# q/k/v and 48-column projections in three rounded passes, with norm sums taken token by token

## The reference

```python
m = silu(c) @ w_mod + b_mod                      # six rows of 1024: shift, scale, gate, twice
h = rms_norm(x, norm1) * (1 + scale) + shift     # latent rows by c, context rows by c_ctx
p = h @ w_in                                     # q k v z | a b | gq gk gv gg | lr
# head group A, gated DeltaNet, 4 heads of 128
q, k, v = split(silu(conv1d_centred(p[qkv], w[3])))
q = q * rsqrt(sum(q*q) + 1e-6) * 128 ** -0.5     # sums over the 128 channels of a head
k = k * rsqrt(sum(k*k) + 1e-6)
# ... chunked scans forward and backward, context first; GLA is head group B ...
x = x + gate1 * (concat(y_a, y_b) @ w_out)
x = x + gate2 * conv_ffn(modulate(rms_norm(x, norm2)))
out = rms_norm(x, final_norm)
```

## Time and profile before

| | |
|---|---|
| median of 3 runs | 1615.28 us (1615.0 to 1617.74) |
| the profiled execution, its own time | 1616.57 us |
| its span, first to last instruction | 1614.8 us |
| mean granted TensorE clock | 0.988 of full speed |
| TensorE, VectorE, ScalarE, GpSimd busy | 97%, 79%, 37%, 31% of the span |
| DMA | 215 MB, mean 133 GB/s |

### The profile page before, as it was taken

The page is one execution under the profiler, slowest core; times in us unless marked ns, Lnnn a source line. Parts: engine busy times, 40 slices in busy tenths (PEclk is TensorE's granted clock), DMA queues, the critical chain, the costliest instruction groups (busy, mean ns, idle before and its releaser), DMA issues.

```text
span 1614.8 us, 20799 instructions
## 1 busy us (share of the span) xinstructions
PE 1572.9 (97%) x8010; PEld 1171.0 (73%) x8010; DVE 1273.6 (79%) x1861; ACT 589.8 (37%) x984; POOL 495.5 (31%) x483
## 2 busy tenths in 40 slices
PE   7999999999999989999999999999999999999997
PEld 2455554987489966565578888888888888788886
DVE  5488878499866678888787389889889888967658
ACT  2544333553243312323464432222222222344455
POOL 5001101121143345656313633433434433600001
PEclk9999999999999989999999999999999999999999
DMA  9276553865398740100433246444352511233365
GB/s 348 74 254 215 179 188 127 255 174 128 93 271 252 210 170 14 27 14 26 148 128 108 88 124 124 124 95 139 75 141 78 119 53 29 88 133 97 101 147 169
DMA packets 216031, 214.99 MB, mean 133 GB/s; under 512 B 41221, under 2 KB 156239, under 8 KB 215708
## 3 DMA queue, kind: packets, MB, share of 16 engines
q1 hardware_dynamic: 200144, 183.97, 36.7%
q0 software_dynamic: 9392, 26.48, 7.5%
q10 hardware_dynamic: 6396, 3.20, 0.7%
HBM read 171.50 MB, written 65.19 MB: 147 GB/s over the span
## 4 chain that ended last, share of the span: by engine, by line
PE 55%; DVE 6%; issue 1%; ACT 1%; POOL 1%; DMA 0%; ACTq 0%; DVEq 0%; POOLq 0%
PE PS L2257 10%; PE PS L2255 10%; PE PS L2259 10%; PE PS L2113 4%; PE PS L2292 4%; PE PS L2294 4%; PE PS L2293 4%; PE PS L2128 3%; DVE Qbd L2587 2%; PE PS L2215 1%; PE PS L2217 1%; PE PS L2216 1%; PE PS L2150 1%; DVE AT L2603 1%; DVE Ex L2568 0%
## 5 line engine op out<-in xcount | busy, mean ns | idle before, releaser
L2758 DVE SCALAR_TENSOR_TENSOR acc<-PS,fcol,acc 128x945 f32<-128x945 f32 (+2 forms) x176 | 215.1, 1222 | 29.2 <-ACT acc L2380 23.7
L2758 DVE SCALAR_TENSOR_TENSOR act<-PS,fcol,act 128x945 f32<-128x945 f32 (+2 forms) x176 | 215.1, 1222 | 21.6 <-ACT act L2380 16.2
L2255 PE MATMUL PS<-h2hi,whi 128*128 128x512 f32 x704 | 219.5, 389 | 0.0
L2259 PE MATMUL PS<-h2hi,wlo 128*128 128x512 f32 x704 | 219.4, 389 | 0.0
L2257 PE MATMUL PS<-h2lo,whi 128*128 128x512 f32 x704 | 219.3, 389 | 0.0
L2024 POOL TENSOR_TENSOR wlo<-wu,whi 128x1024 fp32r<-128x1024 f32 x44 | 106.4, 2423 | 214.1 <-ACT whi L2373 214.0
L425 PE MATMUL PS<-hT,wq 128*128 128x512 f32 (+1 forms) x432 | 163.1, 537 | 0.0
L2259 PEld LDWEIGHTS PS<-h2hi,wlo 128*128 128x128 f32 x704 | 132.1, 188 | 27.5
L2257 PEld LDWEIGHTS PS<-h2lo,whi 128*128 128x128 f32 x704 | 132.1, 188 | 27.4
L2255 PEld LDWEIGHTS PS<-h2hi,whi 128*128 128x128 f32 x704 | 132.1, 188 | 27.4
L425 PEld LDWEIGHTS PS<-hT,wq 128*128 128x128 f32 x432 | 81.6, 190 | 78.4 <-issue 75.6
(11 more groups left out here) (336 smaller groups left out, 2981.0 us busy)
## 6 DMA issues: line engine op xcount, KB each, us to landing
wm<-in_w_mod_dram SPq DMA_DIRECT2D x24, 1024.0 KB, 7.6
wu<-in_w_up_dram SPq DMA_DIRECT2D x44, 512.0 KB, 3.9
t_sums<-in_w_down_dram POOLq DMA_DIRECT2D x12, 1024.0 KB, 9.9
raw<-t_sums SPq DMA_DIRECT2D x44, 256.0 KB, 2.6
raw<-in_w_down_dram SPq DMA_DIRECT2D x33, 256.0 KB, 2.7
wq<-in_w_in_dram SPq DMA_DIRECT2D x12, 512.0 KB, 8.9
gdn_x_image<-ztile SPq DMA_DIRECT2D x10, 516.0 KB, 9.9
gdn_xt_image<-ztile SPq DMA_DIRECT2D x10, 516.0 KB, 8.0
```

The source lines that it names most:

```text
L2255: pe.matmul(PS[:, b + half, :], whi[k][u][:, kk, :], h2hi[:, 4 * half:4 * half + 4, kk, :], start=(kk == 0), stop=False)
L2259: mm = pe.matmul(PS[:, b + half, :], wlo[k][u][:, kk, :], h2hi[:, 4 * half:4 * half + 4, kk, :], start=False, stop=(kk == KT - 1))
L2758: tp = v.scalar_tensor_tensor(out=t_[:, r0:r1, c0:c1], in0=up[:, r0 + dr:r1 + dr, c0 + dc:c1 + dc], scalar=tap_col(j, k, f), in1=t_[:, r0: ...
```

## The change

1. `hT` is no longer built in place. Each tile of h is staged in one of three buffers `hs`, stored to DRAM by SP (`h_out`), rounded by ScalarE into `hhi`, and the rest is subtracted into `hlo`, by VectorE for tiles 0 to 3 and by GpSimd for 4 to 9. A tile reuses the buffer of the tile three before it and waits for its store.
2. The weights of q, k, v and of lrab are split in the same way, `w_high` on ScalarE and `w_low` on GpSimd. Each fp32 matmul becomes three in fp32r (`three`).
3. The product stays in PSUM. ScalarE writes the centre tap from there (`centre`), VectorE adds the two other taps straight from PSUM. The large `raw` buffers go.
4. The squares are summed by using them as weights against one column of ones, in fp32: token sums as a [128, 8] or [128, 10] table (`sums`). Root, reciprocal and turn work on that table; the turned row is stored to DRAM and read back to all partitions (`spread`, on SP). The turn of q's table sits in the v product, that of k's in the next head's q product, after the first 512 columns.
5. v is copied per head into `vst` and stored by ScalarE's queue.
6. The rest of the modulation goes in 32 parts of two steps (0.5 MB each), with two small accumulators that are spilled one by one.
7. At the start of the second stage SP loads ten tiles of `hT` back (5.2 MB) ahead of its other transfers, and the first value weights have their own buffer `wgA`. The third stage loads `hL` in twelve transfers instead of three.

```diff
+                def h_out(t):
+                    sp.wait_ge(s_hta, 2 + t + 1)
+                    sp.wait_ge(s_htv, 2 + t + 1)
+                    sp.dma_start(hT_dram[t], hs[t % 3][:, :, :]).then_inc(s_hst[t % 3], 16)
...
+                def spread(kind, h):
+                    n = NT if kind else NL
+                    sp.wait_ge(s_bank[kind], h + 2)
+                    sp.dma_start(r_dram[kind, h, 0:n, :], nrow[kind][0:n, :]).then_inc(s_nrs[kind], 16)
+                    sp.wait_ge(s_nrs[kind], 16 * (h + 1))
+                    if kind:
+                        sp.wait_ge(s_un[0], h + 1)
+                    elif h:
+                        sp.wait_ge(s_un[1], h)
+                    sp.dma_start(crn[:, 0:n * P], r_dram[kind, h, 0:n, :].rearrange("t p -> (t p)").rearrange("(o n) -> o n", o=1)
+                                .to_broadcast([P, n * P])).then_inc(s_nrb[kind], 16)
...
+                def w_low(kind, h):
+                    g.wait_ge(s_wqh[kind], h + 1)
+                    g.tensor_tensor(wqlo[kind][:, :, :], wq[kind][:, :, :], wqhi[kind][:, :, :], ALU.subtract).then_inc(s_wql[kind], 1)
...
+                def three(out, kind, k, t0, n):
+                    hi, lo = wqhi[kind][:, k, :], wqlo[kind][:, k, :]
+                    pe.matmul(out, hi, hhi[:, k, t0:t0 + n], start=(k == 0), stop=False, skip_group_check=True)
+                    pe.matmul(out, hi, hlo[:, k, t0:t0 + n], start=False, stop=False, skip_group_check=True)
+                    return pe.matmul(out, lo, hhi[:, k, t0:t0 + n], start=False, stop=(k == KT - 1), skip_group_check=True)
...
                 def sums(kind, h):
+                    pe.wait_ge(s_csq[kind], h + 1)
+                    for t in range(NT if kind else NL):
+                        mm = pe.matmul(PS[:, norm_bank(kind), t:t + 1], csq[:, tile_cols(t)], ones[:, 0:1], start=True, stop=True)
                     mm.then_inc(s_css[kind], 1)
...
                 def h_tile(t):
                     u, row = t % 2, t // NL
                     a.wait_ge(s_xt, t + 1)
+                    if t >= 3:
+                        a.wait_ge(s_hst[t % 3], 16 * (t // 3))
...
+                def centre(kind, h):
                     a.wait_ge(s_mm[kind], h + 1)
...
+                    if h == 0:
+                        a.wait_ge(s_xs, NT)
+                        for i in range(3):
+                            a.wait_ge(s_hst[i], 16 * len(range(i, NT, 3)))
+                        a.wait_ge(s_hlp, NT - HLV)
                     b = BANK[kind]
+                    ev = a.activation(cv[kind][:, 0:LAT], PS[:, b:b + 2, :].rearrange("p a n -> p (a n)"), ACT.Copy, scale=tap(1, kind, h))
...
+                def head(h):
+                    parts(8 * h, 8 * h + 2)
+                    if h:
+                        norm_row(1, h - 1)
                     conv(0, h)
+                    if h:
+                        copy_v(h - 1)
+                    parts(8 * h + 2, 8 * h + 4)
+                    if h:
+                        unit(1, h - 1)
                     conv(1, h)
+                    inverse(0, h)
+                    parts(8 * h + 4, 8 * h + 6)
+                    norm_row(0, h)
+                    parts(8 * h + 6, 8 * h + 8)
                     unit(0, h)
                     conv(2, h)
+                    inverse(1, h)
...
-                sp.dma_start(v_dram.rearrange("c p n -> p c n"), vtok[:, :, :]).then_inc(s_vs, 16)
+                for t in range(NT):
+                    sp.dma_start(hT[:, :, tile_cols(t)], hT_dram[t]).then_inc(s_h2[t], 16)
```

More of the change, by code:

```diff
@@ new lines, in _ @@
+                zeros(0)
+                zeros(1)
+                n = 2
+                for h in range(H):
+                    for m, i in enumerate(range(8 * h + 2, min(8 * h + 10, MPARTS))):
+                        if m == 2:
+                            if h:
+                                spread(1, h - 1)
+                            load(0, h + 1)
+                        if m == 5:
+                            load(1, h + 1)
+                        rest(i)
+                        if i % 4 == 2 and i > 4:
+                            sums_out(i // 4 - 1)
+                        if i > 5 and n < 20:
+                            zeros(n)
+                            n += 1
+                        if m == 5:
+                            spread(0, h)
+                    load(2, h + 1)
@@ L423, in product @@
+                def product(kind, h, between=None):
+                    pe.wait_ge(s_wql[kind], h + 1)
+                    if kind == 1:
+                        pe.wait_ge(s_cs[1], 2 * h)
+                    else:
+                        pe.wait_ge(s_bank[kind], h + 1)
                     for b, (t0, n) in enumerate(PARTS[kind]):
+                        if kind == 1 and b == 2:
+                            pe.wait_ge(s_bank[1], h + 1)
                         for k in range(KT):
-                            mm = pe.matmul(PS[:, BANK[kind] + b, 0:n], wq[kind][:, k, :], hT[:, k, t0:t0 + n],
-                                           start=(k == 0), stop=(k == KT - 1))
+                            mm = three(PS[:, BANK[kind] + b, 0:n], kind, k, t0, n)
+                        if b == 0 and between is not None:
+                            turn_norms(*between)
@@ L427, in product @@
                     mm.then_inc(s_mm[kind], 1)
                 def sums(kind, h):
-                    if h == 0 and kind == 0:
-                        pe.wait_ge(s_csq[0], 1)
-                        for b, (t0, n) in enumerate(PARTS[0]):
-                            mm = pe.matmul(PS[:, BANK[0] + b, 0:n], ones[:, :], csq[:, t0:t0 + n], start=True, stop=True)
-                        mm.then_inc(s_css[0], 1)
-                        return
-                    pe.wait_ge(s_onr, 1)
-                    pe.wait_ge(s_csl[kind], h + kind)
@@ L471, in first @@
                             turn(turns[k // 2])
[L472 removed]
+                        mm = three(PS[:, BANK[kind] + b, 0:n], kind, k, t0, n)
                     return mm
+                pe.wait_ge(s_hh, HLV)
+                pe.wait_ge(s_hlv, HLV)
                 first(0, 0, ())
@@ L589, in head @@
+                def head(h):
+                    centre(0, h)
+                    silu(0, h)
+                    if h:
+                        v_out(h - 1)
+                    w_high(0, h + 1)
+                    if h == 1:
+                        a.wait_ge(s_lw, 32)
+                        a.activation(wlrhi[:, :, :], wlr[:, :, :], ACT.Copy).then_inc(s_lrh, 1)
+                    centre(1, h)
                     root(0, h)
                     silu(1, h)
-                    evac(2, h)
+                    w_high(1, h + 1)
+                    centre(2, h)
@@ L707, in copy_v @@
                     cp.then_inc(s_bank[2], 1)
                 def part(i):
-                    g_, kh = divmod(i, 2)
+                    g_, kq = divmod(i, 4)
                     v.wait_ge(s_m2[i % 2], 16 * (i // 2) + 16)
-                    for k in range(4):
-                        kk = 4 * kh + k
+                    m = macc[g_ % 2][:, :]
+                    if kq == 0 and g_ >= 2:
+                        v.wait_ge(s_msp, 16 * (g_ - 1))
+                    for k in range(2):
+                        kk = 2 * kq + k
@@ L721, in head, with parts @@
-                def head(h, last_v):
-                    conv(0, h)
-                    if last_v is not None:
-                        copy_v(last_v)
-                    part(4 * h)
+                            v.tensor_scalar(m, wm2[i % 2][:, k, :], scol[:, kk, 0:1], None, ALU.mult).then_inc(s_ma, 1)
+                def parts(n0, n1):
+                    for i in range(n0, n1):
+                        part(i)
+                def head(h):
+                    parts(8 * h, 8 * h + 2)
+                    if h:
+                        norm_row(1, h - 1)
+                    conv(0, h)
+                    if h:
+                        copy_v(h - 1)
+                    parts(8 * h + 2, 8 * h + 4)
+                    if h:
+                        unit(1, h - 1)
@@ L736, in _ @@
+                for h in range(H):
+                    head(h)
+                norm_row(1, H - 1)
                 copy_v(H - 1)
+                unit(1, H - 1)
                 v.wait_ge(s_hb, 32)
```

401 lines of the change are left out of this document (225 added, 176 removed).

## The result

The changed kernel takes 1637.17 us, the median of 4 runs (1633.94 to 1638.27), against 1616.51 (1615.0 to 1618.42) for the kernel before on the same chip. The ratio is 1.0124, 95% interval 1.0104 to 1.0144: it is slower by some 20 us. The direction was forecast, the size was not (1620, range 1605 to 1634). The profiled execution took 1633.94 us, the fastest of the four, with a span of 1632.1 and a mean granted TensorE clock of 0.973; its span is 17.3 us above the span before.

The account below looks back on a forecast made before the run. The prediction took TensorE to set the pace of the q/k/v stage. Its terms, 16.0 + 1.5 + 3 - 20.4 - 4.3 + 9 = +4.8 us, on the median of 1615.28 gave 1620, range 1605 to 1634.

Parts of the forecast that it names:

- start, to the first value product, with the clock: Staging and stores of h delay the first value product from 85.90 to 101.9, +16.0; TensorE at 1.2 GHz adds 1.5.
- first-head waits and three periods: Norms waiting for a full queue in the first head, +3; head period 51.3 to 44.5 us, three periods -20.4.
- tail of the stage: From the last value product to the second stage, 34.6 us instead of 38.9: -4.3, bounds -6 and -1.
- start of the second stage: Ten h tile loads delay the first value tile about 3 us and the decay tables, +6: +9 together, bounds +4 and +13.
- Products and sums: Per head on TensorE: q product 10.8 us, k and v 13.7 each, norm sums 4.0.
- The waits in the heads: TensorE waits 1.0 us per period for k's inverse, behind q's unit norm and v convolution; first-head norms wait 3.
- the clock: Idle times in the start's chain may return TensorE to 1.2 GHz: +1.5, bounds 0 and 5.
- B: Rival: norm round trip late in every head, TensorE idles in the next q product: 1631, up to 1636; chance 0.20.
- A: Rival: the queue keeps up, no waits in the heads, start +11: -13, 1602; chance 0.19.
- C: Rival: only the start is shorter than forecast, first tile stored sooner: +0, 1615; chance 0.11.
- D: Rival: the products do not speed up, weight loads not hidden: 1640; chance 0.03.
- E: Rival: products run at the skill's 131 ns per matmul of 512 columns: near 1575; chance 0.01.

Follow-up runs that it names:

- E4: Changed kernel, with ScalarE issuing the write of the decay rows and their first six reads in the second stage: 1633.51 us, ratio 1.0106.
- E9: Changed kernel, with VectorE taking k's inverse before q's unit norm and the v convolution: 1625.36 us, ratio 1.0049.
- E15: E9 with the one-column sums of k done twice in each head: 1640.60 us, ratio 1.0142.
- E1: Changed kernel, with the turn of k's inverse norms moved behind the whole q product of the next head: 1624.78 us, ratio 1.0044.
- E3: Changed kernel, with head 0's sums of q after the value product's first 512 columns, the norms' turn after the next 512: 1634.67 us, ratio 1.0107.
- E7: E1 with the first four tiles of h loaded back at the end of the first stage: 1625.31 us, ratio 1.0034.
- E11: E9 with four tiles of h loaded back at the first stage's end and the first value weights loaded where q's weights lay: 1623.52 us, ratio 1.0038.

## Why the prediction was right or wrong

By its own terms, in us against the profile before:

| term | forecast | measured |
|---|---|---|
| start, to the first value product, with the clock | +16.0 + 1.5 | +19.3 |
| first-head waits and three periods | +3 - 20.4 | -9.7 |
| tail of the stage | -4.3 | -3.3 |
| start of the second stage | +9 | +11.4 |
| sum | +4.8 | +17.7 |

**Products and sums: right.** A q product takes 10.8 us without waits, k and v about 13.9, a pass 0.23. The sums take 1.71 for q (247.73 to 249.44) and 2.15 for k, 3.9 together, where 4.0 was summed. The Trainium skill's 131 ns per matmul (TensorE: Matmul & The Clock Gate, Back-to-back issue gap) would have given an estimated 6.3 us for q; the trace disagrees with it, as the rows of the up projection had said.

**The start: right by its steps.** First product 52.2 (52.4), the last tile's low part at about 91 (88.8), first value product 105.25 (101.9), inside the bounds of 97 to 106 given for it. (The chain's own terms, from 91.5 on, add up to 100.6 at the squares and not 100.1; the half microsecond changes nothing.) The two idle times named in it, about 5 and about 6 us, are 5.1 (before the second half of q) and 6.1 (before the sums); a third one, of 2.1 us before the last part of k, was not in it.

**The waits in the heads: right in mechanism, and in size in this execution.** Forecast were 3 us in the first head and 1.0 in each period, 6 in all; measured 5.0 (0.7, 2.7, 1.6), in E4's execution of the same heads 10.0. The mechanism named, k's inverse behind q's unit norm and its round trip, is what E9 undoes. The turn of k stands half of the way into the next q product, not a third, as the prediction and some expectations say.

**The step that failed is the clock.** "I add 1.5, bounds 0 and 5" was put on the start alone. The periods were summed as if TensorE stayed at 2.4 GHz through the heads, since it did in the earlier trace rows. It did not: in the profiled execution 3.4 us at 1.2 GHz in each head cost 1.7 each, 5.1 in the three periods and 1.7 in the tail, and the first value product ran its first 4.4 us at half speed, 2.2 more. With 0.5 per period of products a little longer than summed, less the 1.0 by which the waits were smaller, that is about the 7.7 between -17.4 and -9.7. The new sums were costed as 18 times 0.22 us and nothing was asked about what they do to the engine behind them. E15 shows that they bring the clock down by themselves, in the doubled amount; E1 and E9 show that removing 5 us of waits returns 12; E4 shows that the waits bring it down too. The misses of the other terms are 1.8 at the start, 1.0 in the tail (whose own stretch at 1.2 GHz costs 1.7) and 2.4 in the second stage; against the median, the profiled execution being 3 us under it, the change is some 20. No trace shows these last 3 us; waits like E4's may hold them, which is not shown.

**The second stage: right, at the upper end.** The first tile costs 3.4 (2 to 3 forecast), the wait before the second set of decay products 5.4 (4 to 6), and the first table is taken up 26.5 us into the stage, where it was 16.9 before: 9.6 later for the 8.8 worked out. (The 1.65 us per load there is not "3.9 less 2", which is 1.9; the ten loads and the weight took 17.9 us to issue, 1.63 each.) The 2.4 us above the forecast of 9 fit two stretches of 6.8 us at 1.2 GHz up to 322 us, where the kernel before had one of 3.4 there; no run tests that. The last h tile landed 21.4 us into the stage, a little outside the 18 to 20.

**The rivals.** B came nearest (1631 to 1636). Its chain is there, with round trips of 11 to 12 us in the first three heads, but the waits are 5.0 us in the profiled execution and not the 12 of its 4 us a head; the clock, which it did not name, adds the rest. A, C, D and E are refuted by the value product at 105.25 and the periods of 47.3 to 48.6. The range ended 3 us short: the clock's bound of 5 was laid on the start alone, and the heads had none.

## What to carry to other kernels

When a change puts many instructions with one moving column, or a wait, between dense products, ask for each place what the granted clock was behind the nearest such row, and carry its half-speed stretch as a term per loop iteration, not once. On an in-order engine, look for short results that stand behind an instruction which waits for a transfer: moving one reciprocal of 0.2 us was worth 12 us. And a wait shortened at one place is only worth it if nothing ends a little later: three of the edits here (E3, E7, E11) moved 3 to 9 us to the next wait.

## What was not expected of the hardware

TensorE's clock fell to 1.2 GHz while the engine was busy without a gap, behind 20 (or 40) matmul instructions of one moving column: four times in four with 4.3 us of them, four in four in the changed kernel with 2.15 us, but none in four in E1 with the very same piece, and two in four in E9. Four in four is the extreme: over the 14 profiles with the sums of k in one piece of 2.15 us in every head, a low stretch began within 1.5 us of the end of 22 of 56 pieces. Every other low stretch in these heads, from 112 us on, began in or right behind a wait of TensorE. What decides at 2.15 us is open; the length of the piece alone does not. A write of 4 KB (the norms of q) and its read to all partitions took 11 to 14 us until VectorE used it in the first three heads, and 8 to 9 in the last, whichever engine issued them; from 160 to 200 us the DMA engines were at 86 to 88%.
